# First adaptive norm's shift: condition stationary in four groups of 32 rows, sums by a product with ones

## The reference

```python
c_act = silu(c)
mod = c_act @ ada_w[0] + ada_b[0]            # 1024 x 6144, six rows of 1024
sh1, sc1, g1, sh2, sc2, g2 = split(mod, 6)
h = rms(x) * (1 + sc1) + sh1                 # 512 x 1024
xx = token_shift(h) - h
xs = h + xx * mix                            # six mixtures, one for each projection
r = xs[0] @ w_in[:, 0:1024] ...
```

## Time and profile before

| | us |
|---|---|
| median of 3 runs | 2438.64 (2434.49 to 2443.08) |
| the profiled execution | 2435.84 |
| its span in the profile | 2434.0 |
| TensorE busy | 2378.5 (98%) |
| VectorE busy | 1634.1 (67%) |
| ScalarE busy | 1113.6 (46%) |
| GpSimd busy | 523.3 (22%) |
| chain that ended last: TensorE, VectorE, ScalarE | 77%, 11%, 5% |

### The profile page before, as it was taken

How to read it: one execution, slowest core, us unless ns; L and a number is a source line. 1 busy time by engine, 2 the same in 40 slices (tenths; PEclk the granted TensorE clock), 3 DMA queues, 4 the chain that set the end, 5 groups by cost and what they waited for, 6 DMA issues and landing times.

```text
span 2434.0 us, 38419 instructions
## 1 busy us (share of the span) xinstructions
PE 2378.5 (98%) x16018; PEld 2014.7 (83%) x16018; DVE 1634.1 (67%) x2281; ACT 1113.6 (46%) x1671; POOL 523.3 (22%) x198
## 2 busy tenths in 40 slices
PE   8998989999999999999999999999999999999999
PEld 7747875798989888889898989999887778777787
DVE  6578768896868786488675696666617636777514
ACT  6663545352525445545353454322435435555533
POOL 1312203100000244520000002333134343111233
PEclk9999999999999999999999999999999999999999
DMA  7222344235354344124332323222222222112121
GB/s 297 87 91 66 76 116 180 84 124 189 122 176 170 111 158 138 62 87 148 121 113 88 122 93 120 77 80 70 79 89 102 94 102 102 55 70 70 61 87 69
DMA packets 94412, 264.29 MB, mean 109 GB/s; under 512 B 55200, under 2 KB 55840, under 8 KB 69280
## 3 DMA queue, kind: packets, MB, share of 16 engines
q1 hardware_dynamic: 91936, 253.46, 30.3%
q10 hardware_dynamic: 2304, 8.39, 0.9%
HBM read 256.05 MB, written 5.78 MB: 108 GB/s over the span
## 4 chain that ended last, share of the span: by engine, by line
PE 77%; DVE 11%; ACT 5%; issue 4%; DMA 2%; POOL 1%; SPq 0%; DVEq 0%; ACTq 0%
PE bank L357 13%; PE bank L359 13%; PE bank L358 13%; PE bank L2606 6%; PE bank L2608 6%; PE bank L2609 5%; PE bank L290 2%; PE bank L288 2%; PE bank L289 2%; ACT w_high L378 1%; PE bank L4723 1%; DMA ada_slot<-in_first 1%; PE bank L3321 1%; DVE conv_out L3557 1%; PE bank L4717 1%
## 5 line engine op out<-in xcount | busy, mean ns | idle before, releaser
L388 POOL TENSOR_TENSOR ring_low<-ring,w_high 128x2048 fp32r<-128x2048 f32 (+2 forms) x94 | 426.7, 4540 | 1672.3 <-ACT w_high L378 1672.3
L378 ACT ACTIVATE w_high<-ring 128x2048 fp32r<-128x2048 f32 (+1 forms) x128 | 234.8, 1840 | 227.9 <-PE bank L359 218.4
L357 PE MATMUL bank<-h_high,w_high 128*128 128x512 f32 (+1 forms) x480 | 192.3, 401 | 0.0
L359 PE MATMUL bank<-h_high,ring_low 128*128 128x512 f32 (+1 forms) x480 | 190.2, 396 | 0.0
L358 PE MATMUL bank<-h_low,w_high 128*128 128x512 f32 (+1 forms) x480 | 189.1, 394 | 0.0
L357 PE MATMUL bank<-z_high,w_high 128*128 128x512 f32 x380 | 151.6, 399 | 2.9 <-DVE z_low L4302 1.0
L359 PE MATMUL bank<-z_high,ring_low 128*128 128x512 f32 x380 | 150.3, 396 | 0.0
L358 PE MATMUL bank<-z_low,w_high 128*128 128x512 f32 x380 | 149.6, 394 | 0.0
L2609 PE MATMUL bank<-h_high,ring_low 128*128 128x256 f32 x528 | 147.2, 279 | 0.0
L357 PE MATMUL bank<-hidden_high,w_high 128*128 128x512 f32 x352 | 139.5, 396 | 0.0
L359 PE MATMUL bank<-hidden_high,ring_low 128*128 128x512 f32 x352 | 139.5, 396 | 0.0
(11 more groups left out here) (594 smaller groups left out, 6799.2 us busy)
## 6 DMA issues: line engine op xcount, KB each, us to landing
ring<-in_stream SPq DMA_DIRECT2D x186, 1024.0 KB, 4.8
ada_slot<-in_ada_next SPq DMA_DIRECT2D x40, 512.0 KB, 4.0
ada_slot<-in_gains SPq DMA_DIRECT2D x17, 512.0 KB, 4.5
ada_slot<-in_first SPq DMA_DIRECT2D x16, 512.0 KB, 4.4
scale_weights<-in_first SPq DMA_DIRECT2D x4, 1024.0 KB, 23.1
inverse<-scratch_inverse SPq DMA_DIRECT2D x32, 128.0 KB, 3.1
x_res<-in_x SPq DMA_DIRECT2D x2, 1024.0 KB, 9.0
w_first<-in_first SPq DMA_DIRECT2D x2, 1024.0 KB, 16.7
```

Source lines behind the costliest of these rows:

```text
L357: pe.matmul(out, w_high[:, k, cols], x_high, start=start, stop=False)
L359: return pe.matmul(out, w_low[:, k, cols], x_high, start=False, stop=stop)
L378: act.activation(self.high_buf[:, b % 2, 0:cols], self.c.ring[:, b % SLOTS, 0:cols], ACT.Copy)\
L388: pool.tensor_tensor(self.c.ring_low[:, b % SLOTS, 0:cols], self.c.ring[:, b % SLOTS, 0:cols], self.high_buf[:, b % 2, 0:cols].bitcast(F32 ...
```

## The change

The product is turned round. The column of silu(c) for tile k, repeated 32 times, is stationary (128x32) and writes the rows of `head_group(k)`; the weights of 256 output features move. Tiles k and k+4 add up in the same group of rows, so 8 matmuls leave four partial sums, each in 32 equal rows. VectorE copies these 128x256 numbers to SBUF, times 1/32 (`shift_copy`). TensorE then takes each half of them as stationary and multiplies by a column of ones (`shift_sum`), which adds all 128 rows and turns the row of features into a column. `shift_pair` reads these two columns. Places: the sums of blocks 0 and 1 directly behind their blocks, sum 2 behind k=1, block 3 behind k=2 (before: k=1), sum 3 behind k=3. On VectorE copy 0 stands behind unit tile 0, copy 1 behind `first_low(0)`, copies 2 and 3 before the mixes of tiles 2 and 4. `gemm_done` is raised by 2 at the last matmul of a block.

```diff
+    shift_rows = chip.over("shift_rows", [P, 2 * P], F32, chip.top)
...
+    shift_copied, shift_mm = Step(chip, "rw_shift_copied", 4), Step(chip, "rw_shift_mm", 4)
...
         def shift_block(i):
...
-            for j in range(2):
-                for k in range(KD):
-                    mm = pe.matmul(chip.bank[5 + i % 3][:, j * P:(j + 1) * P], w[:, k, j * P:(j + 1) * P],
-                                   c_col[:, k:k + 1].to_broadcast([P, P]), start=(k == 0), stop=(k == KD - 1))
-                if j == 0:
-                    mm.then_inc(chip.gemm_done, 1)
-            mm.then_inc(chip.gemm_done, 1)
+            for k in range(KD):
+                mm = pe.matmul(chip.bank[5 + i % 3][head_group(k), 0:2 * P], c_col[:, k:k + 1].to_broadcast([P, 32]),
+                               w[:, k, :], start=(k < 4), stop=(k >= 4))
+            mm.then_inc(chip.gemm_done, 2)
+
+        def shift_sum(i):
+            pe.wait_ge(shift_copied.sem, shift_copied.of(i))
+            for j in range(2):
+                mm = pe.matmul(chip.bank[5 + i % 3][:, 2 * P + j:2 * P + j + 1], shift_rows[:, j * P:(j + 1) * P],
+                               chip.ones[:, 0:1], start=True, stop=True)
+            mm.then_inc(shift_mm.sem, 1)
...
         shift_block(0)
+        shift_sum(0)
         chip.keep_warm(pe, 6)
         shift_block(1)
+        shift_sum(1)
...
                     shift_block(2)
             if k == 1:
+                shift_sum(2)
+            if k == 2:
                 shift_block(3)
+            if k == 3:
+                shift_sum(3)
...
+        def shift_copy(i):
+            chip.wait_tile(dve, b_sh + i, 1)
+            dve.tensor_scalar(shift_rows[:, :], chip.bank[5 + i % 3][:, 0:2 * P], 1.0 / 32, None, ALU.mult)\
+               .then_inc(shift_copied.sem, 1)
+
         def shift_pair(i):
             cols = slice(2 * i, 2 * i + 2)
-            chip.wait_tile(dve, b_sh + i, 1)
-            dve.tensor_tensor(chip.mod[:, cols], chip.bank[5 + i % 3][:, 0:2 * P:P], chip.v("ada_b")[:, cols], ALU.add)\
+            dve.wait_ge(shift_mm.sem, shift_mm.of(i))
+            dve.tensor_tensor(chip.mod[:, cols], chip.bank[5 + i % 3][:, 2 * P:2 * P + 2], chip.v("ada_b")[:, cols],
+                              ALU.add)\
                .then_inc(shift.sem, 1)
...
         unit_tile(0)
+        shift_copy(0)
         unit_tile(1)
         shift_pair(0)
         first_low(0)
+        shift_copy(1)
         for k in range(KD):
+            if k in (2, 4):
+                shift_copy(k // 2 + 1)
             mix("r", k)
```

## The result

| | before | changed |
|---|---|---|
| median, 17 runs each | 2436.55 us (2434.43 to 2444.42) | 2449.51 us (2439.93 to 2455.91) |
| the profiled execution | 2435.84 | 2454.88 |
| its span, mean granted clock | 2434.0, 0.995 | 2453.1, 0.988 |

A forecast was written before the change was run, and what follows sets the result against it. The first 60 us were taken as bound by VectorE and ScalarE delivering tiles 4 to 7, not by TensorE. Waits and copies summed to +2.1 us on a median of 2438.64, giving 2440.7, range 2434 to 2446.

The forecast's parts named there:

- What is removed: Four shift blocks on TensorE: 3.6 us each becomes 1.0 us, taking off 10.4 us of work.
- rival (d): In the shift blocks the row groups do not overlap, a block costs 3.6 us: +7.3 us, 2445.9; chance 0.04.
- The copies: Four 128x256 copies from a bank on VectorE, each 0.42 us to the signal and 0.35 us of queue.
- Pair 0, 1, 2: First stage: 0.9 us won, then 0.5 lost waiting for block 1's weights; copy 2 adds 0.35 without a wait.
- Pair 3: VectorE waits for block 3 before the fourth copy; the mix of tile 4 comes 2.2 us late, at 43.1.
- rival (a): TensorE decides the first stage's end, so its saved work comes off: -4.4 us, 2434.2; chance 0.08.
- The sum: First stage: +0.5 + 0.35 + 1.35 - 0.1 = +2.1 us, forecast median 2440.7; chance 0.50.
- Later stages are chained to their predecessors, and I find no wait that would swallow it: Behind the first stage, from 59.13 us: the +2.1 us carries through to the end of the kernel.
- rival (b): New holes before 50 us drop TensorE's clock, costing time before block 3: +3.6 us, 2442.2; chance 0.26.

The follow-up runs named there:

- aligned: The changed kernel with 24 small matmuls at the head of TensorE's program, giving back the 96 missing instructions; ratio to before 1.0012 (0.9999 to 1.0024).
- after_again: The changed kernel once more, unchanged, on the same chip as the controls; ratio to before 1.0051 (1.0031 to 1.0071).
- best: The changed kernel with copies and block 3 moved to avoid VectorE waits, 24 small matmuls at the start, 8 filling matmuls at 374 us; ratio to before 1.0015.

## Why the prediction was wrong, step by step

- *What is removed.* Right: 1.07 us for each block (1.0 taken), so the groups do overlap and rival (d) is out.
- *The copies.* Right: 0.41 and 0.42 us, 0.34 of the queue.
- *Pair 0, 1, 2.* Right: 0.9 us won; a wait of 1.19 us for late weights; copy 2 and sum 2 without a wait.
- *Pair 3.* Right: a wait of 2.42 us (2.1 forecast), mix of tile 4 at 42.57 + 1.1 = 43.7 (43.1). The 0.5 us more is made of small pieces (0.2 at block 1, the rest in TensorE's changes of product).
- *TensorE sets the end*, rival (a): out. In the changed kernel TensorE waits 1.18 us before k=5 for VectorE's remainder.
- *The sum.* +2.1 for the first stage; 1.5 in the profile, 2.6 from the arrival of x, and +2.9 us in the runs of `aligned`, which has the change and the instruction numbers of before. The base of the forecast, 2438.64 from three runs, was 2.1 us above the median of 17.
- *"Later stages are chained to their predecessors, and I find no wait that would swallow it"*: this is the step that failed. I asked whether a later stage would give the 2 us back, and not whether it would be the same stage. The diff takes 96 instructions out of TensorE's stream, and with their numbers given back the cost falls from 0.44% to 0.12% (0.45% with a shift by 256): some 8 of the 10.7 us depend on the place in the stream. With it goes the stop in L1580, 310 us downstream. The row was in the trace of before, with 1.23 us and "issue" as releaser. The sum had no term for it.
- *The clock falls*, rival (b): right as to the engine, wrong as to place and price. I looked for the fall only where the change makes holes and hid it behind the queue (rightly: block 2 lasted 1.94 us from 29.95, and TensorE still waited 0.87 us behind it for `first_low(1)`). The falls that cost lie in later stages, in the profile of the changed kernel above all in the narrow matmuls of the chunk stage: there 17 us at the low level followed a hole of 3.35 us, with TensorE busy 18.98 of 20 us (in after_again, 3.4 us followed one of 1.59).

Left open: why the stop comes at these numbers and in none of the other groups of 256, and what it is; how much of the cost arises at the hole and how much at 940 us; how the rest of `best` arises; and how often the long pass at 940 us comes in the changed kernel.

## What to carry to other kernels

An edit that adds or removes matmuls moves everything behind it in TensorE's instruction stream, and a stop of a us may leave one place and appear in another: before an effect of under 0.5% is put down to the edit, run the old kernel with small instructions at its head that give it the new one's count within 256, and once with 256 of them as a control. Look in the trace for the stretches where TensorE is busy with narrow matmuls and waits beside them: there a filling of 10 matmuls was worth some 7 us. A copy that waits for a transfer belongs behind the work that doesn't need it, even where it only takes 0.4 us.

## What was not expected of the hardware

- A stop of 1.0 to 1.8 us on TensorE that is tied to the number of the instruction: 3777, 4033, 7873 and 8129 in the versions that show it, all equal but for multiples of 256.
- The stop may help. With it, TensorE's idle time before L1751 came as 1.23 and 1.03 us and the clock held; without it, as 3.35 us, and the clock fell.
- 32 moving columns in place of 128 don't shorten the blocks (3.72 us for the first, 3.74 before). From 20 to 25 us TensorE was busy 5.00 us at a granted clock of 0.70, where the kernel before was busy 4.93 us at 1.00.
- VectorE's multiplication with a sum over 1024 columns takes 1.22 us alone, and 4.57 us when it starts during GpSimd's subtraction of 2048 columns (2.9 to 5.5 us at these places in the other profiles).
